# Causal window means by shifted adds on VectorE instead of band matmuls on TensorE

## The reference

```
ug = u.reshape(B, S, POOL_GROUPS, POOL_GC)
cs = concatenate([0, cumsum(ug, axis=1)])
lower = max(t + 1 - win, 0);  count = min(t + 1, win)
pooled = (cs[:, 1:] - cs[:, lower, g]) / count - ug
y = einsum('bsgc,gcd->bsgd', pooled, pool_w) * pool_scale
```

## Time and profile before

| | us |
|---|---|
| median of 3 runs | 2934.84 (2927.94 to 2941.4) |
| the profiled execution | 2934.84 |
| its span | 2932.8 |
| TensorE busy | 2573.5 (88%) |
| VectorE busy | 1458.2 (50%) |
| ScalarE busy | 947.0 (32%) |
| GpSimd busy | 873.2 (30%) |

### The profile page before, as it was taken

The page is one execution under the profiler, slowest core; times in us unless marked ns, Lnnn a source line. Parts: engine busy times, 40 slices in busy tenths (PEclk is TensorE's granted clock), DMA queues, the critical chain, the costliest instruction groups (busy, mean ns, idle before and its releaser), DMA issues. The chain is left out here.

```text
span 2932.8 us, 34862 instructions
## 1 busy us (share of the span) xinstructions
PE 2573.5 (88%) x12407; PEld 2048.4 (70%) x12407; DVE 1458.2 (50%) x3133; ACT 947.0 (32%) x1725; POOL 873.2 (30%) x366
## 2 busy tenths in 40 slices
PE   5998999899899899989968777999996877799999
PEld 4786777678677687767766446878776644687877
DVE  5396342653459633366364545445456454533334
ACT  3333243432333224342233442322223344232221
POOL 2232413233223241323322002344442200234342
PEclk9899999999889999999989798999998879899999
DMA  4222414134312241313432002344432200222232
GB/s 132 74 78 72 153 44 122 47 114 162 109 56 87 65 158 44 109 57 108 151 84 69 1 1 58 122 144 144 158 121 73 69 1 1 58 87 89 91 98 82
DMA packets 133585, 256.03 MB, mean 87 GB/s; under 512 B 23406, under 2 KB 30124, under 8 KB 133420
## 3 DMA queue, kind: packets, MB, share of 16 engines
q1 hardware_dynamic: 133420, 253.81, 27.7%
HBM read 249.58 MB, written 4.19 MB: 87 GB/s over the span
## 5 line engine op out<-in xcount | busy, mean ns | idle before, releaser
L686 POOL TENSOR_TENSOR wl<-raw,wh 128x1024 fp32r<-128x1024 f32 (+2 forms) x362 | 873.0, 2416 | 2031.9 <-ACT wh L1063 2030.7
L756 PE MATMUL ps<-wh,hTh 128*128 128x512 f32 (+4 forms) x1664 | 672.2, 404 | 15.9 <-DVE hTl L1605 15.9
L1063 ACT ACTIVATE wh<-raw 128x1024 fp32r<-128x1024 f32 (+2 forms) x362 | 379.9, 1050 | 863.2 <-PE ps L756 444.4
L756 PE MATMUL ps<-wl,hTh 128*128 128x512 f32 (+4 forms) x1664 | 652.8, 392 | 0.0
L756 PE MATMUL ps<-wh,hTl 128*128 128x512 f32 (+4 forms) x1664 | 652.3, 392 | 0.0
L756 PEld LDWEIGHTS ps<-wh,hTh 128*128 128x128 f32 x1664 | 330.5, 199 | 88.9 <-issue 17.9
L756 PEld LDWEIGHTS ps<-wh,hTl 128*128 128x128 f32 x1664 | 330.3, 198 | 60.9
L756 PEld LDWEIGHTS ps<-wl,hTh 128*128 128x128 f32 x1664 | 331.1, 199 | 53.2
L710 PE MATMUL ps<-cf,arena 128*128 128x128 f32 x800 | 144.0, 313 | 175.7 <-DVE nsm L1573 36.4
L756 PE MATMUL ps<-hTh,wh 128*128 128x512 f32 (+1 forms) x672 | 252.9, 376 | 21.4 <-DVE hTl L1605 13.4
L710 PEld LDWEIGHTS ps<-cf,arena 128*128 128x128 f32 x800 | 108.1, 161 | 219.5 <-issue 78.2
(11 more groups left out here) (262 smaller groups left out, 3311.6 us busy)
## 6 DMA issues: line engine op xcount, KB each, us to landing
raw<-in_w_in_dram SPq DMA_DIRECT2D x160, 512.0 KB, 3.6
raw<-in_w_ff_dram SPq DMA_DIRECT2D x128, 512.0 KB, 3.6
modw<-in_w_mod_dram SPq DMA_DIRECT2D x96, 512.0 KB, 4.7
raw<-in_w_br_dram SPq DMA_DIRECT2D x24, 512.0 KB, 3.7
raw<-in_w_out_dram SPq DMA_DIRECT2D x24, 512.0 KB, 3.6
xm<-in_x_dram SPq DMA_DIRECT2D x8, 512.0 KB, 4.4
raw<-in_w_out_dram SPq DMA_DIRECT2D x16, 256.0 KB, 3.8
raw<-in_w_in_dram SPq DMA_DIRECT2D x8, 408.0 KB, 3.2
```

The costliest lines, as they stand in the source:

```text
L686: pool.tensor_tensor(piece(wl, g % RING, u), piece(raw, g % RING, u), piece(wh, g % SPLIT, u).bitcast(F32), ALU.subtract)\
L756: last = pe.matmul(*args, start=(q == 0 and c == 0 and n_pass == 0), stop=(q == u["quarters"] - 1 and c == u["chunks"] - 1 and n_pass == 2))
L1063: act.activation(piece(wh, g % SPLIT, u), piece(raw, g % RING, u), ACT.Copy)\
```

## The change

`eu` becomes a `feat` unit: the same 96 matmuls of 512 columns per layer, with the operands swapped, so that `uT` has channels on the partitions and tokens along the row. A window mean is then a sum of shifted copies along the row. `pool_band` is gone with its matmuls, its ACT copy and the load of `bands`. The step `pool` begins with a chain on DVE: g + 1 doublings (a small copy of the first 1, 2, 4 or 8 columns, then an add of the row with itself shifted), two small instructions that set the first 16 tokens, one instruction for the other 496, in two of the groups (0 and 2) a small copy, and a one-element memset. The chain takes two slots of `scr`. TensorE's matmul by `pool_w` waits for it.

```diff
-            weave(late, U("eu", E_U, 512, tok(), w="w_in_2", act=("a", l)))
+            weave(late, U("eu", E_U, 512, feat(), w="w_in_2", act=("a", l)))
...
-                if (j, p) == (0, 2):
-                    line.append(("pool_band", l, t))
...
-        elif step[0] == "pool_band":
-            keys = [("scr", step)]
+        elif step[0] == "pool":
+            keys = [("scr", step, 0), ("scr", step, 1)]
...
-        cf = sb("cf", [P, 388])
+        cf = sb("cf", [P, 452])
...
-                    if l == 0:
-                        if 1 in blocks:
-                            sp.wait_ge(product, at("out", layers - 1, "b", TILES - 1))
-                        vl(bands[:], a["bands"])
...
                 elif kind == "pool":
                     _, l, g = step
                     b = bank("aux6", step)
-                    pe.wait_ge(act_result, at("pooled_in", l, g))
+                    pe.wait_ge(dve_result, at("pooled_in", l, g))
                     pe.wait_ge(cmp_loaded, at("poolw", l))
...
-                elif kind == "pool_band":
-                    _, l, g = step
-                    act.wait_ge(product, at("banded", l, g))
-                    act.activation(scratch(("scr", step)), ps[:, bank_of.get(step, 0)], ACT.Copy)\
-                        .then_inc(act_result, mark(act_result, ("pooled_in", l, g), ("free", step)))
...
+                    dve.wait_ge(act_result, at("uT", l, g))
+                    u, src = uT[:, g], uT[:, g]
+                    order = [A[(g + j) % 2] for j in range(g + 1)]
+                    order = order[::-1]
+                    for j, dst in enumerate(order):
+                        sh = 1 << j
+                        dve.tensor_copy(dst[:, 0:sh], src[:, 0:sh]).then_inc(dve_result, mark(dve_result))
+                        dve.wait_ge(dve_result, now(dve_result))
+                        dve.tensor_tensor(dst[:, sh:T], src[:, sh:T], src[:, 0:T - sh], ALU.add)\
+                            .then_inc(dve_result, mark(dve_result))
+                        dve.wait_ge(dve_result, now(dve_result))
+                        src = dst
+                    other = A[0] if order[-1] is A[1] else A[1]
+                    fin = A[0]
+                    dve.tensor_tensor(other[:, 0:16], src[:, 0:16], edge[:, g], ALU.mult)\
...
+                    dve.tensor_tensor(other[:, 0:16], other[:, 0:16], u[:, 0:16], ALU.subtract)\
...
+                    dve.scalar_tensor_tensor(fin[:, 16:T], src[:, 16:T], 1.0 / (2 << g), u[:, 16:T], ALU.mult, ALU.subtract)\
...
+                    if other is not fin:
+                        dve.tensor_copy(fin[:, 0:16], other[:, 0:16]).then_inc(dve_result, mark(dve_result))
+                        dve.wait_ge(dve_result, now(dve_result))
+                    dve.memset(nsm[:, 2, 0:1], 0.0)\
+                        .then_inc(dve_result, mark(dve_result, ("pooled_in", l, g), ("free", keys[1])))
+                    dve.wait_ge(dve_result, now(dve_result))
                     dve.wait_ge(act_result, at("pool_high", l, g))
```

More of the change, by code:

```diff
@@ L420, in build @@
         arena2 = sb("arena2", [P, 48 * 256])
-        cf = sb("cf", [P, 388])
+        cf = sb("cf", [P, 452])
         cb = sb("cb", [P, 640], BF16)
-        with nc.sbuf_tensor("bands", [P, 640], F32) as bands:
-            pass
         maskb = sb("maskb", [P, AT[-1] + WIDTH[-1]], BF16)
@@ L966, in _ @@
                     b = bank("aux6", step)
-                    pe.wait_ge(act_result, at("pooled_in", l, g))
+                    pe.wait_ge(dve_result, at("pooled_in", l, g))
                     pe.wait_ge(cmp_loaded, at("poolw", l))
-                    key = ("scr", ("pool_band", l, g))
-                    pe.matmul(b, poolw[:, g], scr[:, scr_slot[key]], start=True, stop=True)\
-                        .then_inc(product, mark(product, ("pool_out", l, g), ("free", key)))
+                    pe.matmul(b, poolw[:, g], scr[:, scr_slot["scr", step, 0]], start=True, stop=True)\
+                        .then_inc(product, mark(product, ("pool_out", l, g), ("free", ("scr", step, 0))))
                 elif kind == "gate_row":
@@ L1907, in _ @@
                     _, l, g = step
+                    keys = [("scr", step, 0), ("scr", step, 1)]
+                    A = [scr[:, scr_slot[k]] for k in keys]
+                    for k in keys:
+                        if scr_prev[k] is not None:
+                            dve.wait_ge(*place("free", scr_prev[k]))
+                    dve.wait_ge(act_result, at("uT", l, g))
[13 more added lines that the diff above has]
+                    dve.tensor_tensor(other[:, 0:16], src[:, 0:16], edge[:, g], ALU.mult)\
+                        .then_inc(dve_result, mark(dve_result))
+                    dve.wait_ge(dve_result, now(dve_result))
+                    dve.tensor_tensor(other[:, 0:16], other[:, 0:16], u[:, 0:16], ALU.subtract)\
+                        .then_inc(dve_result, mark(dve_result))
+                    dve.wait_ge(dve_result, now(dve_result))
+                    dve.scalar_tensor_tensor(fin[:, 16:T], src[:, 16:T], 1.0 / (2 << g), u[:, 16:T], ALU.mult, ALU.subtract)\
+                        .then_inc(dve_result, mark(dve_result))
+                    dve.wait_ge(dve_result, now(dve_result))
+                    if other is not fin:
+                        dve.tensor_copy(fin[:, 0:16], other[:, 0:16]).then_inc(dve_result, mark(dve_result))
+                        dve.wait_ge(dve_result, now(dve_result))
+                    dve.memset(nsm[:, 2, 0:1], 0.0)\
+                        .then_inc(dve_result, mark(dve_result, ("pooled_in", l, g), ("free", keys[1])))
+                    dve.wait_ge(dve_result, now(dve_result))
                     dve.wait_ge(act_result, at("pool_high", l, g))
@@ L1991, in constants @@
 def constants():
-    cf = np.zeros((P, 388), np.float32)
+    cf = np.zeros((P, 452), np.float32)
     r = np.arange(P)
@@ L2008, in constants @@
     cf[0:N_CMP, 259:387] = rotation(ends)
-    cf[:, 387] = r >= CMP_LEN - 1
-    bands = np.zeros((P, 640), np.float32)
-    ahead = np.arange(144)[None, :] - r[:, None]
     for g in range(4):
[L2013 to L2016, removed]
+        cf[:, 387 + 16 * g:387 + 16 * g + 16] = 1.0 / np.minimum(np.arange(16) + 1, 2 << g)
+    cf[:, 451] = r >= CMP_LEN - 1
     cb = np.zeros((P, 640), np.float32)
@@ L2024, in constants @@
     cb[:, 512:576] = r[None, 0:64] == r[:, None] % 64
-    return {"cf": cf, "cb": cb, "bands": bands, "rot": rotation(np.arange(T))}
+    return {"cf": cf, "cb": cb, "rot": rotation(np.arange(T))}
 def program(draft, nc, arrays, result, **options):
```

9 lines of the change are left out of this document (4 added, 5 removed).

## The result

The changed kernel takes 2962.61 us (median of 4 runs, 2957.84 to 2966.78) against 2932.41 us for the kernel before (4 runs, 2927.94 to 2941.4). The ratio is 1.0094, with a 95% interval of 1.0074 to 1.0114: about 28 us slower. The profiled execution took 2962.29 us, its span 2960.5, 27.7 us longer than before. The forecast of 2945 us and its range up to 2956 were too low.

What follows compares the result with a forecast made beforehand. Pair stages were taken as bound by a dependency chain circling TensorE, VectorE and ScalarE. Bands -18.4, added VectorE work +22.3, clock +4.3 and +2.0, `cf` +0.1: +10.3 us on 2934.84, forecast 2945 us, range 2933 to 2956.

Steps and rivals of the forecast that it cites:

- Where the time goes: Whole kernel: all that is removed and added, apart from `eu`'s other writing and one load, lies in the two pair stages.
- the other writing of `eu`: The 96 matmuls per layer with operands swapped: cost 0, bounds -1 and +1 us.
- The 0.1 us for the longer `cf`: At the kernel's start: 64 more columns of `cf`, 33 KB to load, cost 0.1 us.
- The chain: VectorE in the `pool` steps: 2.50, 3.23, 4.36 and 5.09 us for groups 0 to 3, 15.2 us per layer.
- the rival of dear shifted adds: VectorE's shifted adds take 1.15 us in place of 0.73: 7.6 us more, 2953 us; chance 8%.
- The memset: One-element VectorE instruction in the `pool` step, given 0.20 us like the narrow ones.
- How much of it shows: TensorE's `pool_w` matmul starts later in tiles 1 to 3 of both layers, waiting for VectorE: 22.3 us more.
- Tile 0 is hidden: In tile 0 `gate_row`'s matmuls and ScalarE's copy cover VectorE's added work, with 1.6 us to spare; otherwise 2.65 us.
- The bands: Pair stages: the band matmuls' TensorE time is on the path in full, so removing them gives 18.4 us less.
- The clock behind the stalls: TensorE behind the six new waits in tiles 1 to 3: lower clock costs 5.7 us if all fall, taken as 4.3.
- The 2.0 us for tile 0: Tile 0, both layers: clock may rise later, slowing the `pool` matmul, transposes and logits; 1.0 us each layer.
- slower rival: TensorE stays at 1.2 GHz two more items behind stalls of tiles 1 to 3: 15.4 us more, 2960 us; chance 15%.

Runs made afterwards that it cites:

- filled kernel: Changed kernel plus 11, 13 and 16 unused TensorE matmuls before the wait for the chain in tiles 1, 2 and 3: 2951.02 us, ratio 1.0029.
- without sums: Changed kernel with the VectorE chain deleted and the `pool_w` matmul reading `uT` as it is, window means left out: 2927.31 us, ratio 0.9941.
- a shift of ten matmuls: Ten 512-column matmuls added at the start of each pair stage, in the kernel with neither bands nor chain: 2925.69 us, ratio 0.9975.
- Shifted by ten: Changed kernel with ten 512-column matmuls added ahead of the first matmuls of each pair stage: 2961.73 us, ratio 1.0080.
- both shifts: Changed kernel with ten, or twenty, 512-column matmuls added at the start of each pair stage: 2961.73 and 2974.41 us.
- more of them behind the early chain: Changed kernel, chain two items earlier, unused matmuls ahead of third-, fifth- and seventh-item transposes (12, 4, 5) in tiles 1 to 3: 2924.53 us, ratio 0.9952.
- early chain: Changed kernel with the VectorE chain as its own step two items earlier in all tiles, the `pool_w` matmul kept in place: 2935.12 us, ratio 0.9975.
- before, filled: Kernel before, bands kept, plus twelve unused matmuls ahead of the third item's transposes in tiles 1 to 3: 2934.44 us, ratio 0.9986.

## Why the prediction was wrong

**Where the time goes.** Right. 26.3 of 27.7 us lie in the pair stages. The rest lies outside them: about 2 us less between the two stages and about 4 more behind the second. This is below what two runs of one kernel differ by, so the other writing of `eu` shows no cost. The 0.1 us for the longer `cf` can't be seen in any run.

**The chain.** Right. From the first copy to the matmul's start it takes 3.15, 4.29 and 5.01 us in tiles 1 to 3, against 3.38, 4.51 and 5.24 in the sum. The shifted add takes 0.69 us like the unshifted one in the earlier trace rows, so the rival of dear shifted adds falls. The memset was over-counted, at 0.06 in place of 0.20.

**How much of it shows.** Right. Worked out as in the prediction, from the end of `pair_prob`, the matmul starts 3.36, 4.02 and 3.25 us later in tiles 1 to 3 of layer 0, against 3.67, 4.32 and 3.57. In layer 1 it is 2.46, 4.11 and 3.26 against 2.77, 4.41 and 3.57. The six together are 20.5 us, against 22.3. Tile 0 is hidden. The filled kernel against the one without sums gives 22.8 us for the whole, 21.6 without the fill's overrun.

**The bands.** 18.4 us as instructions; 11.4 in the kernel that leaves them out. The argument "on the path in full" counted what TensorE did and not what its clock would do without it. The loss in tile 2, about 1.4 us a layer, is there in all six stages without sums, and comes behind the 1.4 us of idling. In tile 1 it depends on the moment, and a shift of ten matmuls brings the removal to 286.8 - 268.0 = 18.8 us. The kernel before was not shifted, so how much of the 7 us is its own moment isn't known.

**The clock behind the stalls.** This is the step that failed: "I take three quarters, 4.3 us", out of 5.7 if the clock fell behind every stall. The term is 15.0 us. It priced the matmul by `pool_w` and the one group of transposes and logits behind it: 1.8 or 1.1 us in tile 1, 1.0 in tile 2 and 0.4 in tile 3. Measured against the filled kernel these are 3.8, 2.9 and 1.6 in each layer. The trace after shows 1.2 GHz for 16 us behind the stall of tile 1, with the compressed logits, the value matmuls and the next items in it, and for some 4 us and then 6 in tile 2. The 2.0 us for tile 0 came to nothing: there the `pool` matmul takes 1.13 us and the transposes and logits ahead of it 0.41 and 0.49, before and after alike. The prediction had the clock that stays down as its slower rival, at 2960 us, and gave it 15%. That rival is what happened, though it hit the total by two errors that cancel: with it the clock would have cost 4.3 + 2.0 + 15.4 = 21.7 us, 6.7 more than measured, and the bands brought 7.0 less. The idle stretches shown in the earlier trace rows were read as evidence on whether the clock falls; they said nothing on how long it then stays down. Nor is it the stall that brings the clock down in tile 1 of the changed kernel: it was low already, and the stall comes where it rose in the kernel without sums. Shifted by ten, the stall itself brings it down. What could have warned of long low stretches was in the trace: in tile 0 it was low for `gate_row`'s 16 matmuls and ahead of them.

**The sum as measured.** -11.4 for the bands, +22.8 for the chain on the path, +15.0 for the clock: +26.4 in the stages. That it adds up is no proof, since the terms are differences along one row of kernels (before, without sums, filled, changed). Removing the bands alone gives 7 us more or less with the moment, so the first two terms are good to some 7 us each, in opposite directions; the second has the reading of 20.5 us from the changed kernel's own rows beside it. For the third, the changed kernel holds under both shifts (310.8 and 311.3 are within 2.4 us of 313.2), but the filled one was not shifted, so it too may be off by several us. That it is far above 4.3 us is shown by the ratios as well, 1.0094 against 1.0029 with intervals that don't touch.

**Open.** What the clock looks at isn't known from these runs. That the band matmuls' own work kept the clock up through tile 2's transposes fits all these stages, but no run put other work in their place to show it.

## What to carry to other kernels

In a stage that is bound by a chain going round through several engines, a new wait on TensorE costs its length and then the lower clock on what is behind it, until the clock has risen again: here some 22 us of chain on the path brought some 15 us of clock. So price the whole stretch behind a stall at both clocks, and put new VectorE work where VectorE waits already: the same chain two items earlier costs 32 us less. Matmuls of no use in a stall show by themselves how much of a loss is clock, but before they are kept as a gain they must be measured in the kernel at hand: in the kernel before they made the stages 2.7 us longer, and more of them behind the early chain took back 5.8 us of what the first had brought.

## What the runs showed of the hardware that was not expected

- The granted clock behind one and the same idle stretch is not settled by its length: behind 2.99 us it was 2.4 GHz in one kernel and 1.2 GHz in another whose only difference was 2.1 us of matmuls at the start of the stage, 40 us earlier.
- Once low, it was low for some 16 us in tile 1 of the changed kernel, while TensorE was busy for 2.5 to 5.0 of each 5 us. In tile 3 it rose after some 4 us behind the stall.
- Behind an idle stretch of 1.4 us, too, the clock was low in one kernel (four transposes took 1.08 us in before, filled) and high in another (0.63 in before).
- Removing 32 matmuls a layer and adding waits raised TensorE's busy time, 108.65 to 114.63 us in one stage. Where the clock moves, busy time is no measure of work.
- Adds of a row with itself shifted by 1, 2, 4 or 8 fp32 columns take 0.68 to 0.69 us, like the unshifted ones of the earlier trace rows.
